# Reordering weight splits, silus, logarithms, roots and condition columns in a two-block mixer kernel; upper key heads with unsplit weights, the result stored in four pieces

## The reference, cut to what matters

```python
# first block, per layer
n = rmsnorm(h, norm_g[i])
z = n @ w_in[i] + b_in[i]         # conv value/glu/gate, pool in/gate, q, k, v, attention gate, index q/k/w
ya = conv_module(...) * silu(c_gate)          # 31 taps, layernorm, silu, 256x256 product
yb = pool_mixer(...) * silu(p_gate)
yc = sparse_attention(rope(q), rope(k), v, rope(qi), rope(ki), wi) * silu(a_gate)   # top 64 of 256 keys
h = h + concat([ya, yb, yc]) @ w_out[i]
h = h + (p[i] @ ple_w[i]) * sigmoid(h @ ple_gate_w[i])
# after two layers: rmsnorm(h, final_norm_g)

# second block, per layer, for 256 latent tokens x and 256 context tokens xc (xc updated in layer 0 only)
mod  = silu(c) @ w_ada[layer] + b_ada[layer]              # six shifts, scales and gates; same for c_ctx
u = modulate(rmsnorm(x, g), sh1, sc1) @ w_in[layer]       # GLA q/k/v/low-rank gates/r, short conv, attention q/k/v
gf = log_sigmoid(glr_f @ wg2_fw + bg_fw) / 16             # the gate logarithms; gb likewise
gla = gated linear attention, both directions, its root-mean-square norm, * silu(r)
x = x + g1 * (concat([gla, short_conv, neighbourhood_attention]) @ w_out[layer])
x = x + g2 * conv_ffn(modulate(rmsnorm(x, g), sh2, sc2))  # 1024 -> 2 x 2816 -> 1024
# at the end: rmsnorm(x, final_norm_g)
```

## Time and profile before

| | us |
|---|---|
| median of 3 runs | 1559.84 |
| the profiled execution | 1558.47 |
| its span | 1556.7 |
| PE busy | 1451.4 (93%) |
| PEld busy | 1219.0 (78%) |
| DVE busy | 901.8 (58%) |
| ACT busy | 710.8 (46%) |
| POOL busy | 47.7 (3%) |
| mean DMA rate | 139 GB/s, 216 MB in all |

### The profile page before, as it was taken

One profiled execution on the slowest core, in us unless ns is written; L12 is line 12 of the kernel. 1 busy time (PEld: TensorE's weight loads), 2 busy tenths in 40 slices (PEclk: granted clock), 3 DMA queues, 4 the chain that ended last, 5 costly groups with the idle time before them and its releaser, 6 DMA issues.

```text
span 1556.7 us, 22403 instructions
## 1 busy us (share of the span) xinstructions
PE 1451.4 (93%) x8897; PEld 1219.0 (78%) x8897; DVE 901.8 (58%) x1776; ACT 710.8 (46%) x1200; POOL 47.7 (3%) x65
## 2 busy tenths in 40 slices
PE   5999899998999998899999999999897988999997
PEld 4777887777977876487777778888787875899997
DVE  5597576986733566436555555422523655688854
ACT  4547456365534633524433343322324535466642
POOL 1000000000000012000000000000000210000000
PEclk9999999999999999998999999999998999999998
DMA  6644356334442122622455442332333236565552
GB/s 221 226 135 136 125 164 217 122 108 141 129 162 89 60 95 70 243 81 96 155 173 188 172 137 93 100 96 83 102 120 107 83 95 239 170 190 185 177 186 89
DMA packets 61608, 216.45 MB, mean 139 GB/s; under 512 B 6944, under 2 KB 8992, under 8 KB 61376
## 3 DMA queue, kind: packets, MB, share of 16 engines
...
q10 hardware_dynamic: 144, 0.00, 0.0%
HBM read 213.94 MB, written 1.05 MB: 138 GB/s over the span
## 4 chain that ended last, share of the span: by engine, by line
PE 78%; DVE 9%; ACT 8%; issue 3%; DMA 2%; DVEq 0%; ACTq 0%; SPq 0%
PE bank L559 18%; PE bank L561 18%; PE bank L560 18%; PE bank L529 3%; PE bank L575 3%; ACT WHI L1293 2%; DVE WLO L1809 2%; DMA RAWB<-in_ws 2%; PE bank L618 1%; PE bank L1131 1%; ACT L1293 1%; PE bank L619 1%; PE bank L620 1%; PE bank L597 1%; PE bank L1074 1%
## 5 line engine op out<-in xcount | busy, mean ns | idle before, releaser
L1809 DVE TENSOR_TENSOR WLO<-RAWB,WHI 128x1024 fp32r<-128x1024 f32 (+1 forms) x280 | 333.8, 1194 | 298.7 <-ACT WHI L1293 297.2
L559 PE MATMUL bank<-NHI,WHI 128*128 128x256 f32 (+1 forms) x1440 | 483.3, 336 | 13.9 <-DVE WLO L1809 7.0
L560 PE MATMUL bank<-NLO,WHI 128*128 128x256 f32 (+1 forms) x1440 | 474.3, 329 | 0.0
L561 PE MATMUL bank<-NHI,WLO 128*128 128x256 f32 (+1 forms) x1440 | 474.0, 329 | 0.0
L1293 ACT ACTIVATE WHI<-RAWB 128x1024 fp32r<-128x1024 f32 (+1 forms) x280 | 287.4, 1029 | 215.1 <-PE bank L561 179.6
L559 PEld LDWEIGHTS bank<-NHI,WHI 128*128 128x128 f32 x1440 | 275.6, 191 | 60.2 <-issue 27.2
L560 PEld LDWEIGHTS bank<-NLO,WHI 128*128 128x128 f32 x1440 | 275.7, 191 | 25.1 <-issue 1.9
L561 PEld LDWEIGHTS bank<-NHI,WLO 128*128 128x128 f32 x1440 | 275.6, 191 | 24.3
L1293 ACT ACTIVATE CF<-bank,PRM 128x512 f32<-128x512 f32 (+1 forms) x88 | 59.0, 671 | 198.8 <-PE bank L561 196.4
L2511 DVE SCALAR_TENSOR_TENSOR CF<-bank,PRM,CF 128x510 f32<-128x510 f32 (+1 forms) x88 | 54.2, 616 | 128.2 <-ACT CF L1293 126.8
L559 PE MATMUL bank<-HHI,WHI 128*128 128x512 f32 (+1 forms) x352 | 119.3, 339 | 0.0
...
## 6 DMA issues: line engine op xcount, KB each, us to landing
...
X<-in_xt POOLq DMA_DIRECT2D x1, 1024.0 KB, 7.1
out_x<-X SPq DMA_DIRECT2D x1, 1024.0 KB, 4.8
```

The costliest lines, as they stand in the source:

```text
L559: nc.tensor.matmul(o, hi[:, w], xh, start=(i == 0), stop=False)
L560: nc.tensor.matmul(o, hi[:, w], xl, start=False, stop=False)
L561: ins = nc.tensor.matmul(o, lo[:, w], xh, start=False, stop=(i == slabs - 1))
L1809: V.tensor_tensor(WLO[:, k % SPL, 0:w], RAWB[:, u % RAW, 0:w], WHI[:, k % SPL, 0:w].bitcast(F32), ALU.subtract).then_inc(S("lo_ready"), 1)
```

## The change

- `NATIVE_FROM` moves from `pin` to `kb`: the two upper key tiles of each layer of block 1 are native.
- Starts of block 1's layers: two `rest()` stand ahead of the root (one before and one behind the guess in layer 1), the other two at slabs 2 and 5. The silu of the condition vector moves from ahead of the root to behind the V copies; PE waits for it at the first row units instead of behind `tm`.
- `tm` and `first_values`: in the last of the four units the token tiles go one after the other, each with its own signal `v_made`, and ACT copies each bank as it is signalled.
- PLE stage: ACT's `ple(1)` stands ahead of the splits of YP and of the silus of the convolution; DVE's `rest(2)` ahead of the normalisation.
- Start of block 2's layer 1: `rest()` inside the modulation at slabs 2 and 5, `rest(2)` in place of four behind it.
- Gates: exp and ln stand behind the third unit, ahead of the last wait and the value copies; DVE's combining step one tile earlier.
- End of gated attention: `output_scales` at step 2 and the root on DVE behind the logits of item 1; row groups from step 3 in layer 0 (from step 1 in layer 1, as before); the steps that use the scales one later; `columns(3)` and the modulation that reads it behind output tile 1; output tiles start at bank 0.
- The store goes in four pieces of two slabs.

The diff, cut to its changed lines with a line of context; `first_values` changes as `tm` does:

```diff
@@ -47,7 +47,7 @@
 NZ1 = len(TILES1)
-NATIVE_FROM = Z1["pin"]
+NATIVE_FROM = Z1["kb"]
@@ -396,6 +396,10 @@
                 return (self.tile - 1) % 4
+            def from_bank_0(self):
+
+                self.tile += -self.tile % 4
@@ -433,9 +437,10 @@
                 sp.dma_start(RAWB[:, u % RAW, 0:n], ws[u, :, 0:n]).then_inc(S(f"raw{u % RAW}"), 16)
-            sp.wait_ge(S("x_new"), KS * (DEPTH + 2))
-            sp.dma_start(out, X[:, :, 0:T]).then_inc(S("stored"), 16)
-            sp.wait_ge(S("stored"), 16)
+            for k in range(0, KS, 2):
+                sp.wait_ge(S("x_new"), KS * (DEPTH + 1) + k + 2)
+                sp.dma_start(out[:, k:k + 2, :], X[:, k:k + 2, 0:T]).then_inc(S("stored"), 16)
+            sp.wait_ge(S("stored"), 16 * KS // 2)
@@ -606,18 +611,22 @@
                     hi, lo = unit()
-                    for k in range(2):
+                    if given is not None and u == 3:
+                        pe.wait_ge(S(given), me.nth(given, 2))
+                    for i in range(2 * tts):
+                        k, t = (i // tts, i % tts) if u < 3 else (i % 2, i // 2)
                         s, c = 2 * u + k, slice(k * w, (k + 1) * w)
-                        if given is not None:
+                        if given is not None and u < 3 and t == 0:
                             pe.wait_ge(S(given), me.nth(given))
-                        for t in range(tts):
-                            if s == 0 and b0 + t in held:
-                                pe.wait_ge(*held[b0 + t])
-                            o = bank[b0 + t][:, 0:w]
-                            xh, xl = NHI[:, s, t * P:(t + 1) * P], NLO[:, s, t * P:(t + 1) * P]
-                            nc.tensor.matmul(o, xh, hi[:, c], start=(s == 0), stop=False)
-                            nc.tensor.matmul(o, xl, hi[:, c], start=False, stop=False)
-                            ins = nc.tensor.matmul(o, xh, lo[:, c], start=False, stop=(s == 7))
+                        if s == 0 and b0 + t in held:
+                            pe.wait_ge(*held[b0 + t])
+                        o = bank[b0 + t][:, 0:w]
+                        xh, xl = NHI[:, s, t * P:(t + 1) * P], NLO[:, s, t * P:(t + 1) * P]
+                        nc.tensor.matmul(o, xh, hi[:, c], start=(s == 0), stop=False)
+                        nc.tensor.matmul(o, xl, hi[:, c], start=False, stop=False)
+                        ins = nc.tensor.matmul(o, xh, lo[:, c], start=False, stop=(s == 7))
+                        if s == 7 and t < tts - 1:
+                            ins.then_inc(S("v_made"), 1)
@@ -793,8 +805,6 @@
                 tm(TT, 512, "u_split", beside_values1, b0=6)
-                if l == 0:
-                    pe.wait_ge(S("c_ready"), me.nth("c_ready"))
@@ -956,6 +966,7 @@
                         i = ROWS1.index(t)
+                        pe.wait_ge(S("c_ready"), 1)
@@ -1238,10 +1249,11 @@
                         output_means()
-                    if i == 1:
+                    if i == 2:
                         output_scales()
-                    if i >= 1 and i - 1 < 2 * BESIDE_ROWS[l]:
-                        rows(3, 4 * ((i - 1) % 2), 4 * ((i - 1) % 2) + 4, (i - 1) // 2, BESIDE_ROWS[l])
+                    h = i - (3 if uc else 1)
+                    if 0 <= h < 2 * BESIDE_ROWS[l]:
+                        rows(3, 4 * (h % 2), 4 * (h % 2) + 4, h // 2, BESIDE_ROWS[l])
@@ -1261,10 +1273,12 @@
                 attention(items2(uc), score2, L2, lambda e: (4 + e, 0), pv2, uc, end_of_gated)
-                columns(3, BESIDE_ROWS[l])
                 pe.wait_ge(S("y_split"), me.nth("y_split", 5))
+                me.from_bank_0()
                     fm(KS, n, rhs, "wo_freed", "y_split" if m == 0 else None, 5)
+                    if m == 1:
+                        columns(3, BESIDE_ROWS[l])
@@ -1316,9 +1330,18 @@
                 act.wait_ge(S("unit_done"), me.u)
-            def shift_hi(l, n, shift):
+            def made_values(j, n):
+
+                if j < n - 1:
+                    act.wait_ge(S("v_made"), me.nth("v_made"))
+                else:
+                    act.wait_ge(S("unit_done"), me.u)
+
+            def shift_hi(l, n, shift, rests=()):
                 for s in range(KS):
+                    if s in rests:
+                        rest()
@@ -1417,23 +1440,28 @@
                         split_to((1, 1, 2, 2)[k])
-                    act.wait_ge(S("ld_prm"), 16)
-                    act.wait_ge(S("cv_zeroed"), 1)
-                    A(CV2[:, :, 8:10], prm_col("cvec", 0, 2 * KS).rearrange("p (s c) -> p s c", c=2), ACT.Silu).then_inc(S("c_ready"), 1)
+                rest(2 if l == 0 else 1)
                 guess(GR[:, 0, 0:TT], GR[:, 2, 0:TT], "ms_eps")
+                if l > 0:
+                    rest()
                 for s in range(KS):
-                    if s % 2 == 0:
+                    if s in (2, 5):
                     A(NHI[:, s, T:TC], Y1[:, s, :]).then_inc(S("xh_ready"), 1)
-                act.wait_ge(S("unit_done"), me.u)
                 for t in range(TT):
+                    made_values(t, TT)
+
+                if l == 0:
+                    act.wait_ge(S("ld_prm"), 16)
+                    act.wait_ge(S("cv_zeroed"), 1)
+                    A(CV2[:, :, 8:10], prm_col("cvec", 0, 2 * KS).rearrange("p (s c) -> p s c", c=2), ACT.Silu).then_inc(S("c_ready"), 1)
@@ -1562,12 +1590,12 @@
                 rest()
+                ple(1)
                 ins.then_inc(S("conv_silu"), 1)
-                ple(1)
@@ -1609,13 +1637,14 @@
                     copy_rows(7)
-                    shift_hi(l, TC, SH1)
+                    shift_hi(l, TC, SH1, (2, 5))
                 def values(v):
-                    for t in range(4):
-                        b = (t + 2) % 4 if l == 0 and v == 0 else t
+                    for b in range(4):
+                        t = (b + 2) % 4 if l == 0 and v == 0 else b
+                        made_values(b, 4)
@@ -1687,29 +1716,28 @@
                     act.wait_ge(S("x_split"), me.nth("x_split", KS))
-                    unit(2)
+                    rest(2)
                 else:
-                    unit(4)
+                    rest(2)
                         copy_rows(7)
-                for u in range(4):
+                for u in range(3):
                     unit()
-                    if u >= 2:
-                        gate_abs(2 * u - 4)
-                        gate_abs(2 * u - 3)
+                    if u >= 1:
+                        gate_abs(2 * u - 2)
+                        gate_abs(2 * u - 1)
+                rest()
+                act.wait_ge(S("act_chain"), me.nth("act_chain", 4))
+                A(GTA, GTA, ACT.Exp, scale=-1.0).then_inc(S("act_chain"), 1)
+                act.wait_ge(S("act_chain"), me.nth("act_chain"))
+                A(GTA, GTA, ACT.Ln, bias=1.0).then_inc(S("gln_ready"), 1)
                     tile(i)
-                    if i == 4:
-                        act.wait_ge(S("act_chain"), me.nth("act_chain", 4))
-                        A(GTA, GTA, ACT.Exp, scale=-1.0).then_inc(S("act_chain"), 1)
-                    if i == 5:
-                        act.wait_ge(S("act_chain"), me.nth("act_chain"))
-                        A(GTA, GTA, ACT.Ln, bias=1.0).then_inc(S("gln_ready"), 1)
@@ -1931,11 +1960,14 @@
                             gather_squares(k)
+                rest(2 if l == 0 else 1)
                 rsqrt(*(GR[:, i, 0:TT] for i in (0, 2, 1, 3)), "r_tok")
+                if l > 0:
+                    rest()
                 for s in range(KS + 1):
-                    if s % 2 == 0 and s < KS:
+                    if s in (2, 5):
@@ -2121,11 +2153,11 @@
                 rsqrt(MS1[:, 0, :], MS1[:, 2, :], MS1[:, 1, :], MS1[:, 3, :])
+                rest(2)
                 gated(YP, range(2), 2, 2)
-                rest(2)
@@ -2199,12 +2231,14 @@
                                        ALU.mult, ALU.mult).then_inc(S("x_new"), 1)
-            def modulate(l, n, gain, shift, scale):
+            def modulate(l, n, gain, shift, scale, rests=()):
                 for s in range(KS + 1):
+                    if s in rests:
+                        rest()
@@ -2220,10 +2254,12 @@
                         ins.then_inc(S("x_split"), 1)
-            def residual(l, n, gate, units, sq):
+            def residual(l, n, gate, units, sq, beside=None):
                     rest(units)
+                    if m == 2 and beside is not None:
+                        beside()
@@ -2247,8 +2283,8 @@
                     stats(TC)
-                    modulate(l, TC, f"nmix{l}", SH1, SC1)
-                    rest(4)
+                    modulate(l, TC, f"nmix{l}", SH1, SC1, (2, 5))
+                    rest(2)
@@ -2394,12 +2430,10 @@
                                            ALU.mult, ALU.mult).then_inc(S("og_read"), 1)
-                def output_rsqrt():
-
-                    w = 6 * nt
+                def output_eps():
```

(17 more changed lines are left out.)

29 lines of the change are left out of this document (16 added, 13 removed).

## The result

The changed kernel takes 1504.81 us, the median of 4 runs (1504.57 to 1505.46); the kernel before took 1558.84 in its 4 runs beside them (1557.72 to 1559.95). The ratio is 0.9654, 95% interval 0.9637 to 0.9671: 54 us, or 3.5%, faster. The forecast was 1514, the range 1501 to 1537.

What follows compares the result with a forecast made beforehand. PE was taken as the bound, busy 1451.4 of 1556.7 us, the rest idle stretches with half-clock stretches behind most longer ones. Terms summed to 50.9, less 5 for new slow stretches: 46 us, 1514 for the median, range 1501 to 1537.

Steps and rivals of the forecast that it cites:

- The likeliest case: Whole kernel: the summed terms hold and the time is 1507 to 1522 us; chance 0.50.
- (e): Whole kernel: no new slow stretches and the full figures, 55 us gained, 1505 or below; chance 0.10.
- (c): Whole kernel: semaphores hold the moved work at its old place, so no change, 1559 us; chance 0.02.
- (d): Native tiles' raw buffers stop the weight stream: 1600 us, or 1565 if a third wait; chance 0.03 with like mishaps.
- native tiles: Four upper-key tiles of block 1: PE pays 0.2 to 0.7 each, DVE gets time back; 1 us gained (-2 to +2).
- the deduction of 5 for new ones: Whole kernel: leftover waits move and slow stretches follow them; three of 1.7, 5 us, taken off the sum.
- End of gated attention, layer 1: Waits at scales and columns shrink, with 0.5 of clock: 4.5 us gained (2 to 5.5).
- Layer 0: End of gated attention: waits for scales, DMA, PT and columns shrink, slow stretches go; 12 us gained (6 to 13).
- The starts of block 1: Splits ahead of the root cut PE's idle: 6 us in layer 0 (3 to 8), 3 in layer 1 (1.5 to 4).
- The PLE stage: PE's bank wait of 4.22 becomes 0.5 and its slow stretch goes: 9.5 us for both layers (6 to 10.5).
- The store: End of kernel: with four pieces only the last 256 KB follow the last slab; 2 us gained, at worst 0.
- Logarithms: Gate passes ahead of second value copies end the waits before the sums: 0 and 7.5 us (together 3 to 9).

Runs made afterwards that it cites:

- a_kb_split: The changed kernel with the four upper-key tiles split again instead of native: 1508.36 us against 1503.12 for the changed kernel rerun.
- b_scales: The kernel before plus only `output_scales` at step 2, the root behind the logits and the later steps: 1548.64 us, ratio 0.995.
- b_columns: The kernel before plus only `columns(3)` and the modulation behind output tile 1, output tiles from bank 0: 1541.41 us, ratio 0.991.
- b_ple: The kernel before plus only the PLE edit, `ple(1)` ahead of YP's splits and the silus, `rest(2)` ahead of the normalisation: 1545.0 us against 1556.08, ratio 0.9922.
- b_starts: The kernel before plus only the moved splits and moved silu of block 1's starts: 1550.82 us, ratio 0.996.
- b_values: The kernel before plus the early signal of the value banks and block 2's two splits inside the modulation: 1550.9 us, ratio 0.9973.
- b_logs: The kernel before plus exp and ln behind the third unit and DVE's step one tile earlier, value copies as before: 1552.46 us, ratio 0.9976.
- a_logs_old: The changed kernel with exp and ln back at tiles 4 and 5, DVE's step at tile 6: 1505.87 us, ratio 0.968.
- a_ln_behind: The changed kernel with ln behind the second value copies, exp still ahead of them: 1496.45 us, ratio 0.962.

## Why the prediction held, and where it was off

The likeliest case said 1507 to 1522, and the time is 2 us below it, at the figure of case (e), more than forecast, which had a chance of 0.10; but (e) wanted no new slow stretches, and there were some. Most waits went or stayed as forecast: PE's idle sum fell to 67.9 (forecast about 75), the PLE tile waits 0.80, the sums nothing, tile 4 3.54, and the time at half clock fell by 36%. Rivals (c) and (d) did not come. The native tiles brought no stop of the weight stream: a_kb_split is slower, not faster. The price of (d) was also summed wrong: with a third of the 24 tiles waiting it is 29 less 46, which would be 1543 and not 1565.

**The sum was 8 us short mostly because the terms left out slow stretches that went; the deduction of 5 for new ones was right in kind.** Three did come in new places (232, 461 and 1086), and one grew to 10; by the offsets they cost some 8 us. The one at 1086 stands at a wait of 3.15 that the change does not touch and that has no slow stretch in the kernel before, so it is chance. The stages' gains in the table are net of all this and still sum to 53.2, since more old ones went than the terms had counted: of 20 in the kernel before 11 are left. Among those I had not priced, or not in full, are 3.4 us from 218.6, 3.4 from 1273.3 and the 6.8 from 1283.5. (1 - granted clock) over the span fell from 46 to 30 us. That the total came so near is in part luck.

**End of gated attention, layer 1: 4.5, measured 8.6.** The idle before the scales fell by 2.0 (forecast 2.7) and that at the columns by 1.5 (1.5). Windows of the kernel before, from score 0 to output tile 0 and the slow stretch in it, and a row group of the same stretch of code:

```profile
1278.84:1319.33 40.49, 34.70 (x278) 18.50 (x277) 20.28 (x67) 24.73 (x54) 1.42 (x2) 0.92 0.62 218
1283.50:1290.30 6.80, 4.31 (x32) 2.63 (x32) 4.63 (x17) 4.61 (x9) 1.42 (x2) 0.50 0.17 52
1294.66 1.82 PE L529 MATMUL bank<-RAWB,CV 128*32 128x512 f32 x8
```

The matching window after, 1234.98 to 1267.35, has PE busy 29.86 at full clock. The difference is 4.8, of which the columns that moved out are 1.06. Of the other 3.8, 2.1 is the clock, which the forecast priced at 0.5: the scales take 1.53 in place of 2.83, and the row group behind them 1.06 in place of 1.85. b_scales and b_columns show that this hangs on the wait. The remaining 1.7 is a term that the forecast did not have, row groups late for their DMA. The group at 1294.66 takes 1.82 at full clock where all eight take 1.06 in the changed kernel; its second load landed at 1295.38 and its second half started at 1295.43. The busy figure hides this wait, since the modelled ends of the matmuls cover it.

**Layer 0: 12, measured 9.8** (9.5 alone). The wait for PT, the waits for DMA and those at the columns went as forecast. But the 2.4 for the two waits for DMA was read from one execution: b_ple, b_starts and b_values, with the same code there, wait 0.7 to 0.9. The stretch at the scales did not shorten but grew to 10.

**Two terms were wrong and cancelled.** The starts of block 1 were put at 9 and the native tiles at 1; alone they are 6.2 and 5.2. For the starts I followed the splits only. The moved silu costs its 2.19, which I had, but at the condition rows of layer 1 a load ends last whose landing varies by 1.6 between executions: I had read PE's wait of 0.19 for DMA there and not ACT's 2.16. For the native tiles I priced PE's loss fairly (1.0 measured for a layer's two) and took from DVE's time a good part of the idle but not the slow stretch behind it.

**The PLE stage**, 9.5: measured 9.6 in the two traces and in the single edit, by the chain that was worked out (wait 0.78; forecast 0.5). **The store**, 2: 2.2 and 2.4. That 3.0 of the 4.8 is transfer stood in the forecast without its source; the landing times bear it out, since 768 KB more take 2.2 more, 2.9 for 1 MB. **Logarithms**, 0 and 7.5: the wait of 3 to 3.6 before tile 4 came as forecast, 3.54, the sums wait for nothing, and the stages give -0.7 and 7.5. But the new place of the passes does not earn that alone: b_logs gives 3.7 and a_logs_old 2.3. The slip of the value copies was priced at 0.6 in layer 1 and at nothing in layer 0, and it made the wait at tile 4 2.2 longer in each, with slow stretches in both layers of both kernels; a_ln_behind wins 6.7 of it back. Part of layer 1's gain, 1.15 before tile 4, is the bank order. The drain of 1380 ns that the Trainium skill, "ScalarE: Activation LUTs", section What ACT_TABLE_LOAD costs, puts behind a table load would have made each first copy 2.8 later. The trace again has the pass 0.02 behind the load's end.

**Do the parts add up?** Alone: 12.1 + 6.2 + 3.7 + 4.2 + 21.0, and from the changed kernel 5.2 + 2.4, together 54.8; the whole change gives 54.0. With single intervals of 2 to 3 us each, that the parts add up is compatible with the runs and not more. The traces do show two interactions that cancel in such a sum: the early signal takes out the 1.35 before tile 4 only together with the loop of three units, and the 0.94 behind the first values of layer 1 goes with the signal (b_values) as well as with the bank order (b_columns), so it is counted twice.
